# Experts gathered from x by scaled selections, without a normalised copy, in a two-layer decoder trunk

## Chip, cores and metric

One core of a Trainium2 chip runs the whole program in one launch. The metric is the device time of that core in microseconds. TensorE (PE in the profile) multiplies, VectorE (DVE), ScalarE (ACT) and GpSimd (POOL) do the rest, and SyncE (SP) issues the DMAs.

## The reference, cut to what matters

x is 256 tokens by 1024 features, f32, and there are two layers. A layer is a mixer (an input projection, three attention-like branches, gates, an output projection) and then a hierarchical mixture of experts. The change concerns the second part and the memory that the first leaves to it:

```python
def hier_moe_block(x, norm_g, w_rg, b_rg, w_re, b_re, w1, w3, w2):
    xn = rms_norm(x, norm_g).reshape(n_tok, d)
    g_prob = softmax(xn @ w_rg + b_rg);  g_w, g_idx = top_k(g_prob, 1)
    e_in = (xn @ w_re + b_re) of the chosen group (8 of 32 experts)
    e_w, e_idx = top_k(softmax(e_in), 2)
    hid = silu(xn @ w1[e]) * (xn @ w3[e])        # 32 experts, 256 hidden features each
    hid = hid * combine                          # zero where a token did not choose e
    return x + sum over e of hid @ w2[e]
```

So each token goes through two experts of 32, and all 32 experts have their weights read: 3 x 1 MB each, 96 units of 1 MB for a layer.

## The kernel before

**Mixer.** The input and output projections stream 21 x 2 units of mixer weights through three 8 KB places (ring_a). Each unit is two parts; ACT copies a part to a high half (`split` in run_scalar, L1436), DVE subtracts it for the low half (L1725), and PE multiplies three times (L908 to L910, L924 to L926). SP waits for the low halves (`lo_ready`) before it reuses a place.

**Units of the experts.** A unit is w1, w3 or w2 of one expert, 8 KB in each of 128 partitions. `order` (L522 to L596) lists them in the order of use. 25 places hold them: four are used once (`t.once`, for units 4, 5, 23 and 24) and 21 form a ring (`t.ring`). Nearly all lie over buffers of the mixer, so each becomes free at its own moment: over attention scratch, over xnT, over the gates, over the split buffers, over the merged branches, and `once_x` over x itself, when x has been added into the output sums and copied to xn. `units_ahead` in run_sync (L696 to L750) is the hand-written order of these first loads: each has a wait for what frees its place, and they stand in one queue with the mixer's own loads. After that SP loads unit i of the ring when unit i - 21 of the ring has been used (L781 to L783).

**Routing and gathering.** PE and DVE make logits, pick groups and experts (`choose`), and count, so that each token gets a slot number among 32 slots of each expert it chose (`place`). `select_tile` (L2000) compares slot numbers with places: for a batch of 4 experts, a 0/1 matrix of 128 tokens by 4 x 32 slots, for each of two token tiles (tt). It is written twice into `t.sel[:, tt, pair, again, :]`, so that a transpose of both copies puts the same 64 slots into both halves of the partitions, where the scatter wants them. ACT makes the normalised copy of x, permuted so that the features of one k (those that are k modulo 8) lie side by side:

```python
def x_normalised(tt):                                                        # L1602
    act.wait_ge(rs_ready, tt + 1)
    A(t.xn[tt][:, :].rearrange("p (k q) -> p k q", k=NK), t.x[:, tt, :].rearrange("p (q k) -> p k q", k=NK),
      ACT.Copy, scale=t.rs[:, tt:tt + 1]).then_inc(xn_done, 1)
```

PE gathers the rows of a batch with matmuls whose stationary operand is 128 features of xn and whose moving operand is the selection (`first_gather` L1219 for batch 0, `rows` L1249 for the others), and DVE multiplies by norm2_g on the way out (L2054). The order of features fits the weights: a partition of w1 holds eight neighbouring rows.

**The expert loop.** `steps` (L522 to L594) is one order for all engines. For each expert: `hidden` (L1275; w1 and w3 on four column tiles of 32, L1296), ACT's copy of h (L1650), `hT` (L1398; folding and transposing with h[:, j::2] as stationary operand, L1405), silu and the product with the slot weight. For each pair of experts: `outputs` (w2, L1317), a high and a low half of y, `scatter` into the sums of x with selectT (L1365). Between them lie, for each later batch, four gather steps: two of rows (L1253), the slot weights (L1259) and select_T (L1267), and on DVE the selections of the batch after (`select`, `weigh`). PE waits for each unit with `arrived`. x itself is added into the same sums by `x_to_sums` (L1154).

In the trace one f32 matmul shows as two records, a transpose as one: a call of `rows`, 8 matmuls, is 16 records.

Of the kernel before, what the change touches and what calls it, by code (L numbers as in the profile page):

```python
# [48 lines left out]
ONCE_UNITS = (4, 5, 23, 24)  # L49
# [21 lines left out]

STEPS = [("rows", 0), ("rows", 1), ("weights", 0), ("select", 0)]
# [70 lines left out]
def tensors(nc, ctx):  # L143

    class T:
# [10 lines left out]
    once_x = whole.again().sb("unit_over_x", [P, UNIT])  # L156
# [60 lines left out]
    t.xn = [r.sb("xn_first", [P, D])]  # L217
# [3 lines left out]
    t.wif, t.ifT = r.again().sb("w_if", [P, NK, SLOTS]), Region(nc, r.at + 1024, two.end).sb("if_by_feature", [P, SEQ])  # L221
    units_gate = r.sb("unit_over_gates", [P, UNIT])
    t.xs = r.again().sb("scaled_x", [P, NT, D])
# [6 lines left out]
    unit_scores = whole.again().sb("unit_over_smalls_and_scores", [P, UNIT])  # L230
    whole.part(4 * D)

# [5 lines left out]
    t.xn.append(Region(nc, late.at - 4 * D, late.at).sb("xn_second", [P, D]))  # L238
# [5 lines left out]
    t.ring_a_at, t.split_at, t.merged_at = [9, 11, 12], 13, 19  # L244
# [6 lines left out]
    t.ta, t.tb, t.tw = sb("attn_a", [P, 4, 384]), sb("attn_b", [P, 4, 384]), sb("attn_w", [P, 4, 384])  # L251
    r = three.again()
    t.softplus_hi, _, t.softplus_lo = (r.sb(n, [P, 4, 384], F32R) for n in ("softplus_high", "softplus_r", "softplus_low"))
# [9 lines left out]
    r = late.again()  # L263
    t.xT = r.sb("xT_router", [P, NK // 2, SEQ])
# [174 lines left out]
def layer(nc, t, d, l):  # L439
# [51 lines left out]
    xn_done, rounds_ready = S("xn_done"), S("rounds_ready")  # L491
# [10 lines left out]
    x_in_sums, counts_read = S("x_in_sums"), S("counts_read")  # L502
# [179 lines left out]
    def run_sync(sp):  # L682
# [4 lines left out]
        def split_last(u):  # L687

            sp.wait_ge(lo_ready, 2 * (u + 1))
# [6 lines left out]
        def units_ahead(u):  # L696

            if u == MIX_RING + 4:
                experts_begin(sp)
                load_unit(sp, ring_units[0])  # L700
            elif u == 29:
                sp.wait_ge(mb_t, 1)
                load_unit(sp, ring_units[1])
            elif u == 33:
                sp.wait_ge(mb_s, 2)
                load_unit(sp, ring_units[2])
            elif u == 36:
                sp.wait_ge(part_used, PARTS * FIRST_BRANCH)
                load_unit(sp, ring_units[3])
                load_unit(sp, ring_units[4])  # L710
                sp.wait_ge(mb_o, 2)
                sp.wait_ge(d_ready, 1)
                load_unit(sp, ring_units[5])
            elif u == 37:
                sp.wait_ge(ml_s, 1)
                load_unit(sp, ring_units[6])
            elif u == 39:
                sp.wait_ge(ml_pt, 1)
                load_unit(sp, ring_units[7])
            elif u == 40:  # L720
                sp.wait_ge(wr_ready, 2)
                load_unit(sp, ONCE_UNITS[3])
# [156 lines left out]
    def run_tensor(pe):  # L879
# [351 lines left out]
        def gather_first(tt, banks):  # L1231
            pe.wait_ge(sel_ready, tt + 1)
            pe.wait_ge(xn_done, tt + 1)
            first_gather(tt, banks)
# [12 lines left out]
        x_to_sums(0, 1).then_inc(x_in_sums, 1)  # L1247
# [168 lines left out]
    def run_scalar(act):  # L1416
# [37 lines left out]
        def copy(name):  # L1454
# [13 lines left out]
            elif name in ("mbq", "mbk"):  # L1468
                dst = mbqk[:, int(name == "mbk"), :, :]
            elif name in ("mlq", "mlk"):  # L1470
                o = NC * int(name == "mlk")
                dst = mlpre[:, o:o + NC, 3:]
                src = src.rearrange("p b (c n) -> p (b c) n", n=SEQ)
            else:
                o = 0 if name == "mlo" else NC + 4 * int(name[1:])
                dst = gates[:, o:o + 4, :]
                src = src.rearrange("p b (c n) -> p (b c) n", n=SEQ)
# [50 lines left out]
        def sigmoid(a, b, copied):  # L1528
            act.wait_ge(proj_copied, INDEX[copied] + 1)
            A(gates[:, a:b, :], gates[:, a:b, :], ACT.Sigmoid).then_inc(sig, 1)  # L1530
# [32 lines left out]
        sigmoid(0, NC + NK, "g1")  # L1563
        split(2)
        sigmoid(NC + NK, NC + 2 * NK, "g3"); split(2)
        split(1); copy_w(ml_pt, 1, ml_w); split(1)
        act.wait_ge(ml_prod, 1)
        A(brT[0][:, 2], tb[:, :, 0:256], ACT.Copy).then_inc(out_hi, 1)
        split(2); sigmoid(NC + 2 * NK, NC + 3 * NK, "g5")
# [32 lines left out]
        def x_normalised(tt):  # L1602

            act.wait_ge(rs_ready, tt + 1)
            A(t.xn[tt][:, :].rearrange("p (k q) -> p k q", k=NK), t.x[:, tt, :].rearrange("p (q k) -> p k q", k=NK),
              ACT.Copy, scale=t.rs[:, tt:tt + 1]).then_inc(xn_done, 1)

# [4 lines left out]
        x_normalised(0)  # L1612
# [15 lines left out]
        x_normalised(1)  # L1628
# [83 lines left out]
    def run_vector(dve):  # L1712
# [176 lines left out]
        def merge(b, half):  # L1889
# [5 lines left out]
            o = NC + b * NK + 4 * half  # L1895
# [24 lines left out]
        v.tensor_tensor(tb[:, :, 0:256], psA[:, :, 0:256], gates[:, 0:NC, :], ALU.mult).then_inc(ml_prod, 1)  # L1920
        merge(1, 0)
        dve.wait_ge(out_hi, 5)
        v.tensor_tensor(brT[1][:, 2], tb[:, :, 0:256], brT[0][:, 2].bitcast(F32), ALU.subtract).then_inc(ml_e, 1)
# [76 lines left out]
        def select_tile(n, again, tt):  # L2000

            ex = slice(n * BATCH, (n + 1) * BATCH)
            v.tensor_tensor(t.sel[:, tt, :, again, :].rearrange("p q (e s) -> p q e s", e=2),
                            bc(bc(t.slot_no[:, :], 1, 2), 1, HALF),
                            bc(t.place[:, tt, ex].rearrange("p (q e) -> p q e", e=2), 3, SLOTS),
                            ALU.is_equal).then_inc(sel_ready, 1)
# [20 lines left out]
        select_tile(0, 0, 0)  # L2027
# [3 lines left out]
        select_tile(0, 0, 1)  # L2031
        oh1, oh2 = (b[:, :, :].rearrange(four, g=NG) for b in (t.oh1, t.oh2))

        def select(n, again):

            for tt in range(NT):
                select_tile(n, again, tt)

        def weigh(n, chain, first=False):
            ex = slice(n * BATCH, (n + 1) * BATCH)  # L2040
            dve.wait_ge(sel_ready, NT if first else 2 * NT * (n + 1))
            for tt in range(NT):
                v.tensor_tensor(t.selw[:, tt].rearrange("p (q e) s -> p q e s", e=2),
                                t.sel[:, tt, :, 0, :].rearrange("p q (e s) -> p q e s", e=2),
                                bc(t.comb[:, tt, ex].rearrange("p (q e) -> p q e", e=2), 3, SLOTS),
                                ALU.mult).then_inc(selw_ready, 1)
            if first:
                select(n, 1)
                dve.wait_ge(sel_ready, 2 * NT)
# [33 lines left out]
        with dve.Fori(0, rounds) as r:  # L2083
            for what, arg in steps:
                if what == "selection":
# [3 lines left out]
                    if piece < 2:  # L2089
                        select(n, piece)  # L2090
# [32 lines left out]
            with dve.If(r + 1 < rounds):  # L2123
# [3 lines left out]
                select(0, 0)  # L2127
                select(0, 1)
# [89 lines left out]
```

## Time and profile before

| | us |
|---|---|
| median of 3 runs | 967.45 (966.62 to 967.87) |
| the profiled execution, its own time | 970.34 |
| its span, first to last instruction | 968.6 |
| PE busy | 929.8 (96%) |
| PE's weight loads (PEld) busy | 711.8 (73%) |
| DVE busy | 483.4 (50%) |
| ACT busy | 420.0 (43%) |
| POOL busy | 32.1 (3%) |
| HBM read | 291.05 MB |

PE, PEld, DVE, ACT and POOL are shares of time in which an instruction of the engine was under way; matmuls overlap, so PE at 96% need not be PE at its peak. Layer 1's expert stage runs from about 295 to 486 us, layer 2's from about 776 to 965. Lines (L1253) are those of the kernel before.

### The profile page before, as it was taken

The page shows a single profiled execution, that of the slowest core. Times are in us where ns is not written, and L with a number is a line of the kernel's source. Part 1 is how long each engine was busy: PE and PEld are TensorE (multiplying, and loading weights), DVE is VectorE, ACT ScalarE, POOL GpSimd, SP SyncE. Part 2 cuts the span into 40 slices and gives each one's busy share as a digit, 9 for nine tenths or more (in the row PEclk, how much of TensorE's full clock was granted, in tenths as well). Part 3 has the DMA queues.
Part 4 walks back from the last instruction along what each step waited for, and adds up shares of the span by engine and source line. Part 5 has one row for each costly group of instructions (what it writes and reads, how often), then busy time and mean ns, then how long its engine had stood idle before and what let it go on. Part 6 is the DMA issues. An engine that isn't in the chain of part 4 may idle for free.

```text
span 968.6 us, 17435 instructions
## 1 busy us (share of the span) xinstructions
PE 929.8 (96%) x7170; PEld 711.8 (73%) x7170; DVE 483.4 (50%) x912; ACT 420.0 (43%) x649; POOL 32.1 (3%) x56
## 2 busy tenths in 40 slices
PE   8999999999999999977899999999999999999876
PEld 8898888788796566644598988887887966655543
DVE  6565884577854222222173659755787532223111
ACT  6556654657552221111185566555764522212111
POOL 1010100000000000000010110000000000000000
PEclk9999999999999999999899999999999999999989
DMA  8845455558989999999967255565579899999996
GB/s 269 300 132 174 142 197 168 198 186 323 398 330 390 426 425 425 426 426 426 389 214 260 91 177 179 174 217 181 207 320 398 336 395 425 426 426 425 426 426 259
DMA packets 86304, 293.25 MB, mean 303 GB/s; under 512 B 17040, under 2 KB 17104, under 8 KB 61904
## 3 DMA queue, kind: packets, MB, share of 16 engines
q1 hardware_dynamic: 86224, 292.12, 78.1%
q8 instruction: 58, 0.95, 0.4%
q14 instruction: 22, 0.18, 0.0%
HBM read 291.05 MB, written 1.05 MB: 302 GB/s over the span
## 4 chain that ended last, share of the span: by engine, by line
PE 84%; DMA 12%; ACT 2%; DVE 1%; issue 1%; SPq 0%; POOL 0%; ACTq 0%; DVEq 0%
PE ps_a L908 11%; PE ps_a L910 11%; PE ps_a L909 11%; PE ps_b L1296 10%; DMA unit_over_gates<-in_w_dram 5%; PE ps_b L1317 4%; PE ps_b L1253 4%; PE ps_a L924 4%; PE ps_a L925 4%; PE ps_a L926 4%; DMA units_over_merged<-in_w_dram 3%; PE ps_b L1405 3%; DMA units_over_xnT<-in_w_dram 3%; PE ps_a L1365 3%; PE ps_b L1152 1%; PE ps_b L992 1%
## 5 line engine op out<-in xcount | busy, mean ns | idle before, releaser
L1436 ACT ACTIVATE w_high<-weight_ring 128x1024 fp32r<-128x1024 f32 x166 | 173.9, 1058 | 168.2 <-PE ps_a L910 128.4
L1725 DVE TENSOR_TENSOR w_low<-weight_ring,w_high 128x1024 fp32r<-128x1024 f32 x167 | 200.9, 1229 | 91.6 <-ACT w_high L1436 91.2
L908 PE MATMUL ps_a<-w_high,xnT_high 128*128 128x512 f32 x352 | 140.0, 398 | 0.0
L909 PE MATMUL ps_a<-w_low,xnT_high 128*128 128x512 f32 x352 | 137.2, 390 | 0.0
L910 PE MATMUL ps_a<-w_high,xnT_low 128*128 128x512 f32 x352 | 137.2, 390 | 0.0
L924 PE MATMUL ps_a<-xnT_high,w_high 128*128 128x256 f32 x320 | 91.1, 285 | 0.1
L925 PE MATMUL ps_a<-xnT_low,w_high 128*128 128x256 f32 x320 | 90.5, 283 | 0.0
L926 PE MATMUL ps_a<-xnT_high,w_low 128*128 128x256 f32 x320 | 90.5, 283 | 0.0
L1650 ACT ACTIVATE h<-ps_b 128x256 f32<-128x256 f32 x64 | 24.6, 384 | 143.7 <-PE ps_b L1296 143.7
L908 PEld LDWEIGHTS ps_a<-w_high,xnT_high 128*128 128x128 f32 x352 | 66.1, 188 | 16.2 <-issue 2.8
L910 PEld LDWEIGHTS ps_a<-w_high,xnT_low 128*128 128x128 f32 x352 | 66.1, 188 | 14.1
L909 PEld LDWEIGHTS ps_a<-w_low,xnT_high 128*128 128x128 f32 x352 | 66.1, 188 | 13.4 <-issue 0.5
L2115 DVE TENSOR_TENSOR y_lo<-ps_b,y_hi 128x512 fp32r<-128x512 f32 x30 | 20.7, 691 | 103.4 <-ACT y_hi L1682 103.4
L1405 PEld LDWEIGHTS ps_b<-fold_two_matrices,h 128*128 128x128 f32 x256 | 35.0, 196 | 37.9 <-issue 33.7
L924 PEld LDWEIGHTS ps_a<-xnT_high,w_high 128*128 128x128 f32 x320 | 61.4, 192 | 0.4 <-issue 0.3
L925 PEld LDWEIGHTS ps_a<-xnT_low,w_high 128*128 128x128 f32 x320 | 61.4, 192 | 0.0
L926 PEld LDWEIGHTS ps_a<-xnT_high,w_low 128*128 128x128 f32 x320 | 61.4, 192 | 0.0
L2054 DVE TENSOR_TENSOR XT<-ps_b,gain_by_weight_row 128x512 f32<-128x512 f32 (+1 forms) x32 | 21.6, 675 | 79.6 <-PE ps_b L1253 77.8
L2105 DVE TENSOR_TENSOR h_weighted<-ps_b,slot_weight 128x64 f32<-128x64 f32 x64 | 14.0, 219 | 88.6 <-ACT silu_h L1676 88.6
L1682 ACT ACTIVATE y_hi<-ps_b 128x512 fp32r<-128x512 f32 x30 | 17.9, 598 | 79.4 <-PE ps_b L1317 79.4
L1296 PE MATMUL ps_b<-units_over_splits,XT 128*32 128x256 f32 x512 | 41.8, 411 | 5.6 <-DMA units_over_splits<-in_w_dram 5.6
L1253 PE MATMUL ps_b<-select,xn_first 128*128 128x128 f32 x224 | 47.0, 292 | 0.0
(384 smaller groups left out, 1720.4 us busy)
## 6 DMA issues: line engine op xcount, KB each, us to landing
weight_ring<-in_w_in_dram SPq DMA_DIRECT2D x62, 1024.0 KB, 5.1
units_over_splits<-in_w_dram SPq DMA_DIRECT2D x48, 1024.0 KB, 23.0
units_over_attention<-in_w_dram SPq DMA_DIRECT2D x40, 1024.0 KB, 21.0
weight_ring<-in_w_dram SPq DMA_DIRECT2D x24, 1024.0 KB, 18.9
units_over_xnT<-in_w_dram SPq DMA_DIRECT2D x20, 1024.0 KB, 20.8
units_over_merged<-in_w_dram SPq DMA_DIRECT2D x16, 1024.0 KB, 24.0
weight_ring<-in_w_branch_dram SPq DMA_DIRECT2D x12, 1024.0 KB, 5.1
unit_from_layer_begin<-in_w_dram SPq DMA_DIRECT2D x10, 1024.0 KB, 19.0
```

Source lines behind the costliest of these rows:

```text
L908: mm(pair[:, tt, :], xh, hi[:, k, :], start=row == 0, stop=False)
L909: mm(pair[:, tt, :], xh, lo[:, k, :], start=False, stop=False)
L910: last = mm(pair[:, tt, :], xl, hi[:, k, :], start=False, stop=row == rows - 1)
L924: mm(dst, wh, xh, start=row == 0 and s % 2 == 0, stop=False, skip_group_check=True)
L925: mm(dst, wh, xl, start=False, stop=False, skip_group_check=True)
L926: last = mm(dst, wl, xh, start=False, stop=row == rows - 1, skip_group_check=True)
L1253: last = mm(bank[:, i * P:(i + 1) * P], t.xn[tt][:, k * P:(k + 1) * P], t.sel[:, tt, :, 0, :], start=tt == 0, stop=tt == NT - 1)
L1296: ins = mm(ps_h[c * SLOTS:(c + 1) * SLOTS, :], xT[:, k, slots], units[w][:, k, :], start=i == 0, stop=i == rows_each - 1, skip_group_check ...
L1317: ins = mm(ps_y[c * SLOTS:(c + 1) * SLOTS, :], t.hid[p % 2][:, e, j, :], w2, start=j == 0, stop=j == 1, skip_group_check=True)
L1405: last = mm(ps_x[:, o:o + 2 * SLOTS], t.h[:, j:FE:2], t.fold_two[:, :], start=True, stop=True)
L1436: A(mix_buf(whi, i), mix_raw(i), ACT.Copy).then_inc(hi_ready, 1)
L1725: v.tensor_tensor(mix_buf(wlo, i), mix_raw(i), mix_buf(whi, i).bitcast(F32), ALU.subtract).then_inc(lo_ready, 1)
```

## The change

What it does:

- **No xn.** `x_normalised`, both xn buffers (4 KB each) and the semaphore `xn_done` go. The gathers take `t.x[:, tt, k:D:NK]` as stationary operand, every eighth feature of a row.
- **Scaled selections.** The copy with index 0 of a selection now holds the token's rstd in place of 1: four tensor_scalars of 128x32 (compare, then multiply by rs) for each tile. The copy with index 1 stays 0/1; `weigh` and `select_T` use that one. In batch 0 the 0/1 copy is made before `weigh`'s products, no longer after them.
- **select_T.** Only one copy can be transposed now, so each half of the partitions gets its own matmul with the identity: eight matmuls with 64 columns instead of four transposes of 128.
- **Places.** x must stay, so `once_x` goes, with the wait for `x_in_sums`. The freed 8 KB become a ring place, `unit_merged`, over the gates of merged_by_token: 3 places used once and 22 in the ring, 25 as before. Unit 23 is now loaded as the last of the ring's first lap. `unit_over_scores` moves 4 KB on and waits for `ml_o`; the gates, w_if, ml's product, attn_b and attn_w, and scaled_x lie at other addresses; the last sigmoid becomes two ACTIVATEs.

```diff
-ONCE_UNITS = (4, 5, 23, 24)
+ONCE_UNITS = (4, 5, 24)
+GATES_AT = [NC, NC + 4, NC + 12, NC + 16, NC + 8, NC + 20]
...
-    t.xn = [r.sb("xn_first", [P, D])]
...
+    r = Region(nc, gates_at + UNIT * 4, two.end + 4 * D)
+    unit_merged = r.sb("unit_over_merged_by_token", [P, UNIT])
     units_gate = r.sb("unit_over_gates", [P, UNIT])
...
-    t.once = [once_y[:, :], once_XT1[:, :], once_x[:, :], once_choice[:, :]]
+    t.once = [once_y[:, :], once_XT1[:, :], once_choice[:, :]]
...
-              t.ring_a[:, 2, :]]
+              t.ring_a[:, 2, :], unit_merged[:, :]]
...
             elif u == 39:
-                sp.wait_ge(ml_pt, 1)
+                sp.wait_ge(ml_o, 1)
                 load_unit(sp, ring_units[7])
...
                 load_unit(sp, ring_units[9])
-                sp.wait_ge(merged_lo, 2)
+                sp.wait_ge(merged_lo, 1)
                 load_unit(sp, ONCE_UNITS[1])
                 split_last(40)
                 load_unit(sp, ring_units[11])
+                sp.wait_ge(merged_lo, 2)
+                load_unit(sp, ring_units[13])
                 split_last(41)
                 load_unit(sp, ring_units[12])
...
-                sp.wait_ge(x_in_sums, 1)
-                sp.wait_ge(xn_done, NT)
-                sp.wait_ge(sq_done, 5)
-                load_unit(sp, ONCE_UNITS[2])
...
-                    last = mm(first_bank(k), t.xn[tt][:, k * P:(k + 1) * P], t.sel[:, tt, :, 0, :],
+                    last = mm(first_bank(k), t.x[:, tt, k:D:NK], t.sel[:, tt, :, 0, :],
...
-                    last = mm(bank[:, i * P:(i + 1) * P], t.xn[tt][:, k * P:(k + 1) * P], t.sel[:, tt, :, 0, :],
+                    last = mm(bank[:, i * P:(i + 1) * P], t.x[:, tt, k:D:NK], t.sel[:, tt, :, 0, :],
...
-                    last = tr(bank[:, o:o + P], t.sel[:, tt, j].rearrange("p d s -> p (d s)"), t.ident[:, :])
+                    for half in range(2):
+                        last = mm(bank[half * 2 * SLOTS:(half + 1) * 2 * SLOTS, o:o + P], t.sel[:, tt, j, 1, :],
+                                  t.ident[:, :], start=True, stop=True, skip_group_check=True)
...
-        split(2); sigmoid(NC + 2 * NK, NC + 3 * NK, "g5")
+        split(2); sigmoid("g5", *((GATES_AT[g], GATES_AT[g] + 4) for g in (4, 5)))
...
-        def select_tile(n, again, tt):
+        def select_tile(n, scaled, tt):
...
+            if scaled:
+                for i in range(BATCH):
+                    e = n * BATCH + i
+                    ins = v.tensor_scalar(t.sel[:, tt, i // 2, 0, i % 2 * SLOTS:(i % 2 + 1) * SLOTS], t.slot_no[:, :],
+                                          t.place[:, tt, e:e + 1], t.rs[:, tt:tt + 1], ALU.is_equal, ALU.mult)
...
         def weigh(n, chain, first=False):
             ex = slice(n * BATCH, (n + 1) * BATCH)
-            dve.wait_ge(sel_ready, NT if first else 2 * NT * (n + 1))
+            if first:
+                select(n, False)
+            dve.wait_ge(sel_ready, 2 * NT * (n + 1))
...
-                                t.sel[:, tt, :, 0, :].rearrange("p q (e s) -> p q e s", e=2),
+                                t.sel[:, tt, :, 1, :].rearrange("p q (e s) -> p q e s", e=2),
```

## Rows read from the trace of the kernel before

**Rows 1.** page, part 2: what the DMA moved, GB/s in 40 slices of the span
```profile
GB/s 269 300 132 174 142 197 168 198 186 323 398 330 390 426 425 425 426 426 426 389 214 260 91 177 179 174 217 181 207 320 398 336 395 425 426 426 425 426 426 259
```

**Rows 2.** busy us by stage: window, length, PE, PEld, DVE, ACT, POOL, PEclk, DMA, GB/s
```profile
305.00:400.00 95.00, 95.00 (x1048) 58.93 (x1044) 27.27 (x86) 19.09 (x53) 0.00 (x0) 1.00 1.01 425
400.00:474.90 74.90, 62.09 (x633) 37.95 (x632) 13.81 (x45) 11.93 (x33) 0.00 (x0) 0.93 1.01 425
...
880.00:954.10 74.10, 62.34 (x636) 38.72 (x635) 13.81 (x45) 12.24 (x34) 0.00 (x0) 0.93 1.01 425
```

**Rows 3.** chain of waits in the expert stages: start us, us, what
```profile
305.33 1.98 PE ps_b L1253 x16
...
403.94 26.37 DMA unit_over_gates<-in_w_dram
...
460.30 3.22 PE ps_b L1296 x32
...
470.15 1.86 PE ps_b L1296 x32
...
474.94 2.02 PE ps_b L1317 x16
...
909.41 3.00 PE ps_b L1296 x32
```

**Rows 4.** waits of PE, 395 to 480: us in total, times, longest
```profile
PE ps_b L1405 <- ACT h L1650: 0.6, 1, 0.6
```

**Rows 5.** weight loads by line: ns min/median/max, first and last start, form
```profile
L1253 PEld LDWEIGHTS ps_b<-select,xn_first x224: 186/192/333, 305.3 to 930.9; 128*128 128x128 f32 x112
...
L994 PEld LDWEIGHTS ps_b<-attn_w,sb_v x32: 137/137/138, 75.7 to 595.5; 128*64 128x64 f32 x32
...
L1296 PEld LDWEIGHTS ps_b<-weight_ring,XT x192: 106/110/110, 313.3 to 916.5; 128*32 128x32 f32 x192
...
L1405 PEld LDWEIGHTS ps_b<-fold_two_matrices,h x256: 192/196/197, 297.9 to 956.4; 128*128 128x128 f32 x128
```

**Rows 6.** groups by line and form, ACT and DVE: busy us, mean ns, idle before
```profile
L1605 ACT ACTIVATE xn_first<-x_res,rstd 128x1024 f32<-128x1024 f32 x2 | 4.4, 2212 | 0.1
...
L1498 ACT ACTIVATE scaled_x<-mb_qk 128x1024 f32<-128x1024 f32 x4 | 4.0, 1047 | 0.0
...
L407 DVE TENSOR_REDUCE fold<-ident 128x32 f32<-128x128 f32 x1 | 0.4, 370 | 0.0
...
L2003 DVE TENSOR_TENSOR select<-slot_no,place 128x128 f32<-128x128 f32 x64 | 16.0, 287 | 1.1
```

**Rows 7.** a small DVE group; PE's timeline before the second count
```profile
L2050 DVE TENSOR_SCALAR place<-place 128x8 f32<-128x8 f32 x16 | 2.6, 166 | 0.1
...
290.96 0.19 PE L1206 MATMUL ps_b<-assigned,ones_bf 128*128 128x32 bf16 x1 [0.21 <-DVE assigned L1991]
```

**Rows 8.** PE's timeline, values weighed by head, select_T: start us, us, line
```profile
75.43 0.66 PE L992 MATMUL ps_b<-attn_w,sb_v 128*64 128x256 f32 x4
...
76.93 0.50 PE L908 MATMUL ps_a<-w_high,xnT_high 128*128 128x512 f32 x1
...
297.61 0.60 PE L1267 MATMUL ps_b<-ident,select 128*128 128x128 f32 x4
298.04 0.58 PE L1405 MATMUL ps_b<-fold_two_matrices,h 128*128 128x64 f32 x4
```

**Rows 9.** SP's timeline of DMA issues around the start of the expert stage
```profile
267.74 6.04 SPq L625 DMA_DIRECT2D weight_ring<-in_w_dram  x2
...
295.29 0.33 SPq L625 DMA_DIRECT2D unit_over_x<-in_w_dram  x1
297.18 0.33 SPq L625 DMA_DIRECT2D unit_from_layer_begin<-in_w_dram  x1
```

**Rows 10.** the stretch before the expert stage, both layers; columns of rows 2
```profile
273.00:281.00 8.00, 8.00 (x58) 7.36 (x57) 1.96 (x4) 4.39 (x10) 0.00 (x0) 1.00 0.67 218
753.00:761.00 8.00, 8.00 (x56) 7.30 (x55) 2.18 (x4) 4.39 (x11) 0.00 (x0) 1.00 0.65 223
```

More of the change, by code:

```diff
@@ L155, in tensors @@
     sb = whole.sb
-    once_x = whole.again().sb("unit_over_x", [P, UNIT])
     t.x = sb("x_res", [P, NT, D])
@@ L220, in tensors @@
     t.selT = [r.sb(f"selectT{i}", [P, HALF, SEQ], F32R) for i in range(2)]
-    t.wif, t.ifT = r.again().sb("w_if", [P, NK, SLOTS]), Region(nc, r.at + 1024, two.end).sb("if_by_feature", [P, SEQ])
+    at = gates_at + 12 * SEQ * 4
+    t.wif, t.ifT = Region(nc, at, two.end).sb("w_if", [P, NK, SLOTS]), Region(nc, at + 1024, two.end).sb("if_by_feature", [P, SEQ])
+    r = Region(nc, gates_at + UNIT * 4, two.end + 4 * D)
+    unit_merged = r.sb("unit_over_merged_by_token", [P, UNIT])
     units_gate = r.sb("unit_over_gates", [P, UNIT])
-    t.xs = r.again().sb("scaled_x", [P, NT, D])
+    t.xs = Region(nc, r.at - 4 * D, two.end).sb("scaled_x", [P, NT, D])
     once_y = r.again().sb("unit_over_y", [P, UNIT])
@@ L250, in tensors @@
     sb = three.again().sb
-    t.ta, t.tb, t.tw = sb("attn_a", [P, 4, 384]), sb("attn_b", [P, 4, 384]), sb("attn_w", [P, 4, 384])
+    t.ta, t.tw, t.tb = sb("attn_a", [P, 4, 384]), sb("attn_w", [P, 4, 384]), sb("attn_b", [P, 4, 384])
     r = three.again()
-    t.softplus_hi, _, t.softplus_lo = (r.sb(n, [P, 4, 384], F32R) for n in ("softplus_high", "softplus_r", "softplus_low"))
+    t.softplus_hi, t.softplus_lo = (r.sb(n, [P, 4, 384], F32R) for n in ("softplus_high", "softplus_low"))
     sb = spare.sb
@@ L263, in tensors @@
     r = late.again()
+    t.product = r.again().sb("ml_product", [P, NC, SEQ])
     t.xT = r.sb("xT_router", [P, NK // 2, SEQ])
@@ L1246, in run_tensor @@
         x_to_sums(0, 0, [1])
-        x_to_sums(0, 1).then_inc(x_in_sums, 1)
+        x_to_sums(0, 1)
         def rows(bank, q):
@@ L1526, in if_softplus, with sigmoid @@
             A(lft[:, :, :], lft[:, :, :], ACT.Ln, bias=1.0).then_inc(if_sp, 1)
-        def sigmoid(a, b, copied):
+        def sigmoid(copied, *ranges):
             act.wait_ge(proj_copied, INDEX[copied] + 1)
-            A(gates[:, a:b, :], gates[:, a:b, :], ACT.Sigmoid).then_inc(sig, 1)
+            for a, b in ranges:
+                last = A(gates[:, a:b, :], gates[:, a:b, :], ACT.Sigmoid)
+            last.then_inc(sig, 1)
         split(4); copy("sbq"); split(4); copy("sbk"); split(4); copy("sbv")
@@ L1562, in run_scalar @@
         rows_exp(d_ready, 1, False, w_ready)
-        sigmoid(0, NC + NK, "g1")
+        sigmoid("g1", (0, NC + NK))
         split(2)
-        sigmoid(NC + NK, NC + 2 * NK, "g3"); split(2)
+        sigmoid("g3", (GATES_AT[2], GATES_AT[3] + 4)); split(2)
         split(1); copy_w(ml_pt, 1, ml_w); split(1)
         act.wait_ge(ml_prod, 1)
-        A(brT[0][:, 2], tb[:, :, 0:256], ACT.Copy).then_inc(out_hi, 1)
-        split(2); sigmoid(NC + 2 * NK, NC + 3 * NK, "g5")
+        A(brT[0][:, 2], t.product[:, :, :], ACT.Copy).then_inc(out_hi, 1)
+        split(2); sigmoid("g5", *((GATES_AT[g], GATES_AT[g] + 4) for g in (4, 5)))
         nc.scalar.preload_act_table_set(EXP_LN)
@@ L1600, in run_scalar @@
               ACT.Copy).then_inc(xT_act, 1)
[L1602 to L1606, printed above, removed]
         experts_begin(act)
@@ L1611, in run_scalar @@
         rstd(0, msum_ready, rs_ready)
-        x_normalised(0)
         def exps(tt):
@@ L1627, in run_scalar @@
         rstd(1, msum_ready, rs_ready)
-        x_normalised(1)
         exps(1)
@@ L1919, in run_vector @@
         dve.wait_ge(ml_o, 1)
-        v.tensor_tensor(tb[:, :, 0:256], psA[:, :, 0:256], gates[:, 0:NC, :], ALU.mult).then_inc(ml_prod, 1)
+        v.tensor_tensor(t.product[:, :, :], psA[:, :, 0:256], gates[:, 0:NC, :], ALU.mult).then_inc(ml_prod, 1)
         merge(1, 0)
         dve.wait_ge(out_hi, 5)
-        v.tensor_tensor(brT[1][:, 2], tb[:, :, 0:256], brT[0][:, 2].bitcast(F32), ALU.subtract).then_inc(ml_e, 1)
+        v.tensor_tensor(brT[1][:, 2], t.product[:, :, :], brT[0][:, 2].bitcast(F32), ALU.subtract).then_inc(ml_e, 1)
         split(2); merge(1, 1)
@@ L1998, in place @@
                                             in1=t.A[:, tt, :], op0=ALU.add, op1=ALU.mult))
-        def select_tile(n, again, tt):
[L2002 to L2006, printed above, removed]
+        def select_tile(n, scaled, tt):
[4 more added lines that the diff above has]
+                                          t.place[:, tt, e:e + 1], t.rs[:, tt:tt + 1], ALU.is_equal, ALU.mult)
+            else:
+                ex = slice(n * BATCH, (n + 1) * BATCH)
+                ins = v.tensor_tensor(t.sel[:, tt, :, 1, :].rearrange("p q (e s) -> p q e s", e=2),
+                                      bc(bc(t.slot_no[:, :], 1, 2), 1, HALF),
+                                      bc(t.place[:, tt, ex].rearrange("p (q e) -> p q e", e=2), 3, SLOTS),
+                                      ALU.is_equal)
+            ins.then_inc(sel_ready, 1)
         third, last = slice(CHUNK, CHUNK + 256), slice(CHUNK + 256, D)
@@ L2026, in run_vector @@
         place(0)
-        select_tile(0, 0, 0)
+        select_tile(0, True, 0)
         ch.until(logits_out(1))
@@ L2030, in run_vector, with select @@
         place(1)
-        select_tile(0, 0, 1)
+        select_tile(0, True, 1)
         oh1, oh2 = (b[:, :, :].rearrange(four, g=NG) for b in (t.oh1, t.oh2))
-        def select(n, again):
+        def select(n, scaled):
             for tt in range(NT):
-                select_tile(n, again, tt)
+                select_tile(n, scaled, tt)
         def weigh(n, chain, first=False):
             ex = slice(n * BATCH, (n + 1) * BATCH)
-            dve.wait_ge(sel_ready, NT if first else 2 * NT * (n + 1))
+            if first:
+                select(n, False)
+            dve.wait_ge(sel_ready, 2 * NT * (n + 1))
             for tt in range(NT):
                 v.tensor_tensor(t.selw[:, tt].rearrange("p (q e) s -> p q e s", e=2),
-                                t.sel[:, tt, :, 0, :].rearrange("p q (e s) -> p q e s", e=2),
+                                t.sel[:, tt, :, 1, :].rearrange("p q (e s) -> p q e s", e=2),
                                 bc(t.comb[:, tt, ex].rearrange("p (q e) -> p q e", e=2), 3, SLOTS),
                                 ALU.mult).then_inc(selw_ready, 1)
-            if first:
-                select(n, 1)
-                dve.wait_ge(sel_ready, 2 * NT)
             chain.after(v.tensor_scalar(t.place[:, :, ex], t.place[:, :, ex], -float(SLOTS), None, ALU.add))
@@ L2089, in run_vector @@
                     if piece < 2:
[L2090 removed]
+                        select(n, piece == 0)
                     else:
@@ L2126, in run_vector @@
                 dve.sem_clear(go_dve)
-                select(0, 0)
-                select(0, 1)
+                select(0, True)
+                select(0, False)
                 first_rows()
```

16 lines of the change are left out of this document (7 added, 9 removed).

## The prediction

> **What bounds the kernel now.** I read the slices of the page first, then the chain of waits, then the engines' busy time by stage. The slices show two stages for each layer: a mixer, in which the DMA moves 130 to 270 GB/s, and an expert stage, in which it moves 425 GB/s from end to end [rows 1]. In the first 95 us of the expert stage both PE and the DMA are full; in its last 75 us the DMA still moves 425 GB/s, while PE is busy for 62.1 us of 74.9 (62.3 of 74.1 in layer 2) [rows 2]. The chain agrees: it leaves PE at 403.94 for transfers and comes back to PE for good only at 460, after which the last w2 units are fetched [rows 3]. So PE first lives on the units loaded ahead, uses them up, and then takes each unit as it lands. The end of the stage is set by the moment at which the DMA has moved 96 units of 1.05 MB, and PE has about 13 us in hand. How much exactly: idle 74.9 - 62.1 = 12.8 us, less 0.6 us in which it waits for ACT's copy of h [rows 4], plus 1.4 us that one group of hidden matmuls loses to a lower granted clock after an idle stretch (3.22 us, where such a group takes 1.86; 3.00 in layer 2) [rows 3]. That is 13.6 us in layer 1 and 11.8 - 0.6 + 1.1 = 12.3 us in layer 2. A change gains here if it makes DMA work start sooner, and costs nothing until it has added those 13 us to PE's work. This change does some of both.
>
> **The stationary operand read with a stride.** Every gather of rows (L1253, L1226) now loads 128 values that lie 32 bytes apart in x, where xn had them side by side. Nothing in the trace loads PE in that way, so I bound it. A load of 128 columns takes 192 ns, of 64 columns 137, of 32 columns 110 [rows 5]: 0.85 ns a column beside a fixed part, 109 ns in all, and a call of 16 records takes 1.98 us, 124 ns each [rows 3], so the load paces the record and whatever it grows by is added in full. Lower end: no growth. Upper end: h is loaded with every second value (8 bytes apart) and takes 196 ns, 4 more [rows 5]; two of its values share 16 bytes, so a fresh 16 bytes cost at most 113 / 64 = 1.77 ns, and 128 of them 226 ns, 117 more than now. Two neighbours show what such a stride costs other engines. ACT's x_normalised reads x with just this stride: 2212 ns, where a copy of 1024 values side by side takes 1047, so 1.14 ns more for each value. DVE's reduction that builds fold reads values 128 bytes apart: 370 ns for 128 values, where another pass over 128 takes 287, so 0.65 ns more [rows 6]. Both pay, and h's 4 ns are what 1.77 ns for each fresh 16 bytes would give. I take 0.8 ns a value, between DVE's and the upper end (0.91): 102 ns for each record. Per layer there are 7 batches of 2 calls of 16 records, 224 x 0.102 = 22.8 us. The first batch's 32 records stand before the stage on PE's path: 3.3 us, of which the 0.2 us that PE waits before L1206 now hides some [rows 7]: 3.1.
>
> The Trainium skill speaks against this change too: "Advanced Engine Details and Errata", section "SBUF Cachelines", says that SBUF is read in 16-byte lines, that two hits on a line are needed to hide its latency, and that a new line with each access is penalised. It gives no size. By that rule the loads get dearer; were it not to hold for PE's weight loads, the second case below would be the forecast. The ACT and DVE rows agree with it, and no row before the change shows it for PE.
>
> **select_T.** Four transposes become eight matmuls of 64 columns, 16 records. Today's four take 0.43 us from start to next start. The nearest rows are the 16 records of L992 and L994, of the same 128*64 form on alternating halves, with 8 x 256 + 8 x 128 = 3072 columns in 1.50 us, 0.49 ns a column [rows 8]; 16 x 128 columns give 1.0 us. That is 0.57 us more for each of 8 batches, 4.6 us a layer. Ends: 0.3 us if the halves overlap better, 1.3 us if they don't overlap at all.
>
> **DVE.** A scaled tile is four tensor_scalars where one tensor_tensor of 287 ns [rows 6] was. A small tensor_scalar takes 166 ns [rows 7], pipelined less: 0.4 to 0.7 us for the four, so 0.1 to 0.4 more before PE's first gathers. The unscaled selections of batch 0 now stand before weigh, 0.5 us, and slot_weights waits for them right after the first hidden group. Together 0.5 us on PE's path. In the loop the six further instructions run while PE does a hidden group of 1.86 us; uncovered they would cost 0.5 us a batch.
>
> **At nothing.** x_normalised (2 x 2.2 us of ACT a layer) goes: the first is done long before its use, the second ends while DVE still chooses; what is late next is the selection. One more ACT instruction for g5 falls into idle time before the next split. The unit over the scores waits for ml_o instead of ml_pt; two w_out transfers issued just ahead cover that, and without them 1 to 2 us of DMA idle would come out of the second case's gain alone.
>
> **The extra place.** A unit goes out at 268 instead of unit_over_x at 295.29 [rows 9]. From 273 to 281 the DMA has a busy share of 0.67 (0.65 in layer 2), so 2.6 to 2.8 us idle [rows 10]; one unit is 1.05 MB at 425 GB/s, 2.5 us, and fits. Against it, nothing is queued between the last merged unit and the first reused place at 297.18, 1.9 us later than x's unit [rows 9]: 0 to 1.9 us of idle come back; I take 0.8. Net 1.7 us a layer, if the DMA still sets the end.
>
> **The sum.** PE's added work a layer: 22.8 + 3.1 + 4.6 + 0.5 = 31.0 us. That is more than PE has in hand, so the DMA's gain is worth nothing and PE sets the end: 31.0 - 13.6 = 17.4 and 31.0 - 12.3 = 18.7, together 36 us. The profiled execution took 970.34 us, 2.9 over the median of the runs shown, so 1006.4 by its own time and **1003 us** by the median.
>
> **The cases.** About 0.2% (1.9 us) can be told from no change.
> 1. Strided loads pay about double (0.50): 1003. Its own range is 988 to 1012: 83 ns a record (DVE's extra) and 0.3 us for select_T give 23.9 us a layer at the lower end, 117 ns a record 34.9 at the upper (halves that don't overlap would add 6 us a layer to that).
> 2. Strided loads are free (0.34), the case on the other side. PE's extra is 4.6 + 0.5 us, below the 12 to 13 in hand, the DMA sets the end, and the filled gap is worth 1.7 us a layer: 964. It decides as long as a record grows by less than (12.3 - 5.1) / 256 = 28 ns. For it: a load asks for a value each 0.85 ns, which may be slow enough to hide a fresh line each time, and h pays 4 ns only. Against it: the ACT and DVE rows.
> 3. Free loads and no gain (0.08): the idle time at 273 comes back in full where unit_over_x was (1.9 us), or behind the wait for ml_o: 967.
> 4. Loads dearer by about 55 ns (0.08): 14.1 + 5.1 = 19.2 us, less what is in hand, +5.6 and +6.9: 980.
>
> Faster 0.34, same 0.08, slower 0.58. The range for 8 in 10 must take in the first two: 963 to 1010; a little of the free case lies below it, and the dearest form of the first above.
>
> **What would show it.** Right: PE's weight loads of x_res for the gather near 290 ns instead of 192, a call of 16 records near 3.6 us, PE without waits for transfers after 400, and the DMA's share falling below 1 well before the stage ends. Wrong: loads of 192 to 220 ns; then PE still waits for units from about 400 on, the DMA's idle time at 273 is gone, and the last w2 group starts 1 to 2 us sooner in each layer. select_T near 1 us would confirm its term, 1.7 us would say that the halves don't overlap. Wrong in another way: PE waits before its first gathers of more than 0.5 us, or a wait for the selections in the loop.

## The result, and the profile after

The changed kernel takes 1030.14 us (median of 4 runs, 1028.46 to 1030.49) beside 967.25 for the kernel before (4 runs, 966.62 to 967.87): 1.0647 times as long, 95% interval 1.0633 to 1.0660. The direction was predicted, the size was not: 62.9 us slower where 36 were forecast, and outside the range. The profiled execution took 1030.34 us, its span is 1028.6.

PE now reads x with the stride. The loads and matmuls of the gather in the expert stage, over both layers, against the 192 ns of L1253 [rows 5]; then PE's waits over the span, longest sums first (us in total, times, longest):

```profile
L1251 PEld LDWEIGHTS ps_b<-select,x_res x448: 312/336/340, 311.2 to 993.5; 128*128 128x128 f32 x150
L1251 PE MATMUL ps_b<-select,x_res x448: 401/402/505, 311.2 to 993.7; 128*128 128x128 f32 x150
```

```profile
PE ps_b L1251 <- DVE select L1999: 10.9, 12, 0.9
PE ps_b L1383 <- DVE hid L2109: 2.9, 2, 1.5
PE ps_b L1405 <- ACT h L1644: 2.3, 4, 0.6
...
PE ps_b L1225 <- DVE select L1999: 1.2, 4, 0.3
```

A load takes 336 ns, 144 more. A call of 16 records grows by 2.03 us (1.98 before [rows 3], 4.01 where nothing waits ahead of it, as at 344.88 below), 127 ns a record. Nothing waits for a transfer of weights any more; in its place stands a wait for DVE's scaled selections, 0.9 us in 12 of the 14 batches gathered in the loops. The chain of waits shows what surrounds one of them (start us, us, what):

```profile
332.27 0.63 PE ps_b L1405 x4
...
332.92 0.23 ACT silu_h L1670
...
333.25 0.24 DVE h_weighted L2105
...
333.51 0.24 DVE hid L2109
...
333.77 1.76 DVE select L1999 x8
335.53 0.14 issue
335.66 4.16 PE ps_b L1251 x16
339.82 2.58 PE ps_b L1317 x16
...
344.88 4.01 PE ps_b L1251 x16
```

DVE first has to finish the expert of the moment (h_weighted, hid), and only then makes eight selections of 0.22 us each. PE's hidden group runs meanwhile, from 332.8 to 334.75, and is over 0.8 us before the last of them. The gather's call behind the wait takes 4.16 us, and the w2 group behind it 2.58 us. That second number is the clock. Stretches of 2.5 us of the same batch, and the stages (columns of rows 2):

```profile
335.00:337.50 2.50, 1.84 (x8) 1.87 (x8) 0.52 (x3) 0.28 (x1) 0.00 (x0) 1.00 1.02 426
337.50:340.00 2.50, 2.50 (x14) 2.23 (x17) 0.14 (x1) 0.00 (x0) 0.00 (x0) 0.57 1.01 426
340.00:342.50 2.50, 2.50 (x17) 0.48 (x10) 0.55 (x1) 0.00 (x0) 0.00 (x0) 0.74 1.02 433
342.50:345.00 2.50, 2.50 (x37) 1.50 (x37) 1.54 (x5) 0.72 (x2) 0.00 (x0) 1.00 1.01 426
...
337.90:341.20 3.30, 3.30 (x16) 2.03 (x19) 0.69 (x1) 0.00 (x0) 0.00 (x0) 0.50 1.00 425
...
273.00:281.00 8.00, 8.00 (x60) 7.43 (x58) 1.57 (x4) 2.75 (x8) 0.00 (x0) 1.00 0.89 349
281.00:305.00 24.00, 23.24 (x174) 19.94 (x177) 12.40 (x83) 5.27 (x17) 0.00 (x0) 0.93 0.71 270
305.00:400.00 95.00, 91.68 (x866) 60.57 (x859) 26.39 (x93) 15.52 (x43) 0.00 (x0) 0.95 0.99 409
400.00:505.60 105.60, 102.28 (x977) 68.28 (x977) 25.70 (x88) 16.79 (x48) 2.32 (x2) 0.95 0.88 364
...
1000.00:1015.00 15.00, 14.42 (x176) 9.91 (x176) 1.95 (x7) 2.92 (x8) 0.00 (x0) 1.00 0.00 1
```

After 11 of the 12 waits (not after the first of layer 2), about 2 us into the strided call, the granted clock falls to half (0.50, the level of 1.2 GHz) for over 3 us; here from 337.9 to 341.2. It is at half once more just ahead of the stage, from 290.1 to 293.4 in layer 1. The DMA's share in the second part of the stage is 0.88, where it was 1.01 [rows 2], and from 1000 to 1015, in the last 30 us of layer 2, it moves next to nothing: the end is PE's. The gap at 273 is mostly filled (0.89 for 0.67 [rows 10]).

### The profile page after: what moved, and what is told of

It reads as the page before. It is cut to its first block, busy times and chain, and to the rows that moved or that the text cites. A ratio compares the mean times of both kernels' runs of the same rounds, so it can differ in the third digit from the quotient of the medians.

```text
span 1028.6 us, 17905 instructions
## 1 busy us (share of the span) xinstructions
PE 1002.1 (97%) x7362; PEld 779.3 (76%) x7362; DVE 503.9 (49%) x1008; ACT 411.1 (40%) x647; POOL 31.1 (3%) x56
## 4 chain that ended last, share of the span: by engine, by line
PE 92%; DVE 4%; ACT 2%; issue 1%; DMA 1%; POOL 0%; SPq 0%; ACTq 0%; DVEq 0%
PE ps_b L1251 11%; PE ps_a L907 11%; PE ps_a L909 10%; PE ps_a L908 10%; PE ps_b L1296 9%; PE ps_b L1317 6%; PE ps_a L923 4%; PE ps_a L924 4%; PE ps_a L925 4%; PE ps_b L1405 4%; PE ps_a L1365 3%; DVE select L1999 2%; PE ps_b L1225 2%; PE ps_b L1266 2%; PE ps_b L1151 1%; PE ps_b L1257 1%
## 5 line engine op out<-in xcount | busy, mean ns | idle before, releaser
L1251 PEld LDWEIGHTS ps_b<-select,x_res 128*128 128x128 f32 x448 | 108.9, 334 | 23.8 <-issue 22.1
L1251 PE MATMUL ps_b<-select,x_res 128*128 128x128 f32 x448 | 115.0, 417 | 10.9 <-DVE select L1999 10.9
L1670 ACT ACTIVATE silu_h<-ps_b 128x64 f32<-128x64 f32 x64 | 14.3, 223 | 102.8 <-PE ps_b L1405 102.8
## 6 DMA issues: line engine op xcount, KB each, us to landing
weight_ring<-in_w_dram SPq DMA_DIRECT2D x24, 1024.0 KB, 10.9
```

Of the source, the lines that this page charges most:

```text
L1251: last = mm(bank[:, i * P:(i + 1) * P], t.x[:, tt, k:D:NK], t.sel[:, tt, :, 0, :], start=tt == 0, stop=tt == NT - 1)
```

## Experiments

Each comparison has its own runs of the kernel before: 967.57 us (13 runs) for the first four below, 966.83 (15 runs) for the adjacent kernel with one-pass selections and for the three that move the order to the weights, 967.16 (11 runs) for the three between them.

**The changed kernel without the stride.** It gathers 128 adjacent features of x, so other ones than the reference's.

```diff
-    t.x[:, tt, k:D:NK]
+    t.x[:, tt, k * P:(k + 1) * P]
```

> The changed kernel, but its gathers take 128 features of x that lie side by side, so other features than those the weights want. Theory S (the stride of the stationary operand is the cost): a weight load is back at 192 ns and a call of 16 records at 2.0 us. PE then has only select_T (about 4.7 us a layer), the waits for the four tensor_scalars (5.5 us a layer) and a later start (2 us) on top of before, about the 12 to 13 us that it had in hand, so the DMA or PE sets the end by a hair: 963 to 971 us. Rival X (the gathers are slow because of what they read or multiply, x's buffer or the rstd in the selections, not because of the stride): loads stay at 335 ns and the time near 1030 us.

Measured: 969.08 us, 1.0018 (1.0004 to 1.0032). All but 2 us of the 63 go with the stride, and yet PE waits for DVE as often and as long as in the changed kernel. Waits of PE from 303 to 500 us:

```profile
PE ps_b L1251 <- DVE select L1999: 5.5, 6, 0.9
PE ps_b L1296 <- DMA units_over_splits<-in_w_dram: 2.4, 1, 2.4
...
```

These waits come out of what PE has in hand, and so cost next to nothing here (with one-pass selections and no such waits the time is the same, below). That is also why this run alone can't price the stride: it removes the cause that makes everything else count.

**The kernel before with the stride.** `t.xn[tt][:, k:D:NK]` in both gathers, all else as before; other features than the reference's.

> The kernel before, but its gathers take every eighth value of xn, so other features than those the weights want; nothing else of the change. Theory S: each call of 16 records takes 4.0 us in place of 1.98, 14 x 2.0 + 2 x 2.2 = 32.5 us a layer, less the 13 that PE has in hand: +39 us, 1006 us. If the clock also falls after each strided call without any wait for DVE ahead of it, 4 to 5 us a layer more: 1015 us. Rival X: no change in the loads and 967 us.

Measured: 999.51 us, 1.0325 (1.0304 to 1.0346). PE's added work is 28 calls of 2.03 us and the first gathers, which let the stage begin 3.4 us later (298.63 for 295.26): 56.8 + 6.8 = 63.6 us. The time rose by 31.9, so PE had 31.7 us in hand, 15.8 a layer, where 13 were expected. The granted clock is 1.00 from 330 to 480: strided calls alone don't bring it down.

**The law of the stride.** In the kernel before, block k of the gather in the loop is read at a stride of k + 1 values, each from its own line (L1255 for stride 1 to L1269 for stride 8); other features than the reference's.

```diff
-    t.xn[tt][:, k * P:(k + 1) * P]
+    t.xn[tt][:, 0:127 * (k + 1) + 1:k + 1]
```

> The kernel before, with feature block k of each later batch read from xn at a stride of k + 1 values (4 to 32 bytes), a line of the source for each, so that each line's load time can be read; other features than the weights want. Theory S with 16-byte lines: 192 ns at a stride of 1, 196 at 2, between at 3, and about 335 ns alike at 4 to 8, since each value then lies in a 16-byte line of its own. Rival: the load grows in proportion to the distance, about +20 ns for each step. Rival: it doubles already at 2 or 3.

Measured: 973.44 us (one run). Weight loads from xn_second, ns min/median/max:

```profile
L1255 PEld LDWEIGHTS ps_b<-select,xn_second x28: 192/192/192, 305.2 to 927.0; 128*128 128x128 f32 x28
L1257 PEld LDWEIGHTS ps_b<-select,xn_second x28: 196/196/197, 305.7 to 927.4; 128*128 128x128 f32 x28
L1259 PEld LDWEIGHTS ps_b<-select,xn_second x28: 261/261/261, 306.3 to 928.1; 128*128 128x128 f32 x28
L1261 PEld LDWEIGHTS ps_b<-select,xn_second x28: 330/330/330, 307.1 to 928.9; 128*128 128x128 f32 x28
L1263 PEld LDWEIGHTS ps_b<-select,xn_second x28: 314/314/314, 310.4 to 934.4; 128*128 128x128 f32 x28
L1265 PEld LDWEIGHTS ps_b<-select,xn_second x28: 318/318/318, 311.3 to 935.2; 128*128 128x128 f32 x28
L1267 PEld LDWEIGHTS ps_b<-select,xn_second x28: 326/326/326, 312.2 to 936.2; 128*128 128x128 f32 x28
L1269 PEld LDWEIGHTS ps_b<-select,xn_second x28: 334/335/336, 313.2 to 937.1; 128*128 128x128 f32 x28
```

A stride of two values (8 bytes) costs 4 ns, three cost 69 ns, and from four (16 bytes) on the load is at 314 to 335 ns. It doesn't grow in proportion to the distance: what counts most is how many values lie in the same 16 bytes. The spread of 21 ns among the strides from four up is not explained by that. The time agrees with the stock of 32 us: the two calls of a batch take 2.74 and 3.84 us from start to next start, 2.62 more than 2 x 1.98, which is 36.7 us for 14 batches, and the kernel got 5.9 us slower, so 30.8 us were hidden. (The mean extra of the eight loads is 91 ns, and 448 of that would be 41 us: the calls grow by nine tenths of what the loads grow.)

**The changed kernel with one-pass selections.** The scaled copy is made of the 0/1 copy by one multiplication of 128x128 with rs for each tile: four DVE instructions a batch where there were ten. Everything is computed.

```diff
-                for i in range(BATCH):
...
-                    ins = v.tensor_scalar(t.sel[:, tt, i // 2, 0, i % 2 * SLOTS:(i % 2 + 1) * SLOTS], t.slot_no[:, :],
-                                          t.place[:, tt, e:e + 1], t.rs[:, tt:tt + 1], ALU.is_equal, ALU.mult)
+            dve.wait_ge(sel_ready, count)
+            v.tensor_scalar(t.sel[:, tt, :, 0, :], t.sel[:, tt, :, 1, :], t.rs[:, tt:tt + 1], None, ALU.mult)
```

> The changed kernel, but the scaled selection of a tile is made from the 0/1 one by one multiplication of 128x128 by rstd, not by four comparisons of 128x32. Theory D (the tensor_scalars of 0.22 us each make PE wait, and each wait with the strided call behind it brings PE's clock down once a batch): the 5.5 us of waits and the six or seven stretches at the lower clock (0.7 us each) go in each layer, 18 to 20 us in all: 1011 us. Rival: the new chain of comparison and multiplication is as late as the old one, or the clock falls from the strided call alone: 1020 to 1030 us.

Measured: 1008.91 us, 1.0435 (1.0410 to 1.0459), 21.2 us less than the changed kernel, with the stride in place. A batch in its chain:

```profile
331.38 1.86 PE ps_b L1296 x32
333.24 0.05 issue
333.30 4.04 PE ps_b L1251 x16
337.34 1.85 PE ps_b L1317 x16
...
354.25 1.02 PE ps_b L1266 x16
```

No wait for the selections, w2 groups at 1.85 us, mean clock 1.000 over the span. So the small selections cost 21 us once PE sets the end: 10.9 us of waits, 11 times the 0.85 us of a fallen clock (4.16 - 4.04 and 2.58 - 1.85), 9.4 us, and 1.8 us at the start of the two stages (the first hidden group begins at 300.1 for 298.9 in layer 1; in layer 2 at 809.4 for 797.2, of which 11.65 come from layer 1), 22.1 in all. Over the strided kernel before it stands 9.4 us. select_T is 7.3 us of that: a call takes 1.02 us here, and there 0.59 us in 14 calls of 16 and 0.44 in the first of each layer. One of the 14, in the chain of the strided kernel before:

```profile
327.57 0.59 PE ps_b L1267 x4
```

The other 2.1 us are not accounted for; the runs of either kernel spread over 3.3 us.

**Adjacent and one pass: what is left is the place.** Both edits above together; other features than the reference's.

> The changed kernel with both suspected costs taken away at once: each gather reads 128 adjacent features of x (so other features are gathered than the reference wants), and the scaled selection of a batch is one 128x128 multiplication of the 0/1 one per token tile. What is left of the change is the ninth unit place, the missing copy and the longer select_T. Theory A (stride 61 us, DVE selections the rest, the place worth about 1.7 us a layer where the queue sets the end): no wait of PE for DVE select, the waits for DMA units back, 964 to 965 us. Theory B (the place is worth nothing, since select_T and the fuller ring only move the wait): 967 to 968 us. If the DVE waits cost nothing in the adjacent form either, it reads 969 like the adjacent kernel with eight small selections.

Measured: 968.07 us, 1.0014 (1.0005 to 1.0024). No gain, though the gap at 273 is filled. The next two runs say why.

**The kernel before, profiled again.**

> The kernel before, profiled a second time. Its first profiled execution lies 2.9 us over the median of its times, so places gained and lost by a few us can't be read against it. Theory A (the extra place is worth 1.7 us a layer, the profile of the adjacent form with two-pass selections shows it): the last w_dram unit of the first expert stage lands near 460 here too. Theory B (the first profiled execution was a slow one, and the place is worth nothing): it lands at 458 to 459, and the time is 966 to 968 us.

Measured: 966.35 us (one run). So its first profiled execution was on the long side, and small differences are to be read against this one. The two stretches around the place, of this kernel:

```profile
273.00:281.00 8.00, 8.00 (x58) 7.39 (x57) 1.78 (x4) 4.42 (x9) 0.00 (x0) 1.00 0.68 219
281.00:305.00 24.00, 23.20 (x236) 17.77 (x234) 12.99 (x84) 9.54 (x23) 0.00 (x0) 1.00 0.98 386
```

and of the adjacent kernel with one-pass selections:

```profile
273.00:281.00 8.00, 8.00 (x57) 7.35 (x57) 1.91 (x4) 3.06 (x9) 0.00 (x0) 1.00 0.88 360
281.00:305.00 24.00, 23.39 (x241) 18.26 (x243) 12.95 (x84) 6.15 (x20) 0.00 (x0) 1.00 0.91 351
```

DMA idle before: 8 x 0.32 + 24 x 0.02 = 3.0 us. After: 8 x 0.12 + 24 x 0.09 = 3.1 us. What is won at 273 is idle again where unit_over_x used to be fetched: from 295 to 300 the DMA's share is 0.55, and 0.92 in the kernel before. There are 25 places before and after; the change moves one of them.

**One place fewer.** The same kernel without `unit_merged` in the ring, 24 places; other features than the reference's.

```diff
-              t.ring_a[:, 2, :], unit_merged[:, :]]
+              t.ring_a[:, 2, :]]
...
-                load_unit(sp, ring_units[13])
```

> The adjacent form with two-pass selections, with the new place (the unit over merged by token, issued at 268) taken out again, so that no unit is loaded into the memory of the missing copy at all; features other than the reference's are gathered. Theory A (where the queue sets the end, a place filled before the stage is worth up to its transfer of 2.5 us a layer): 971 to 973 us. Theory B (places are worth nothing here): 967 to 968 us, as with it.

Measured: 973.04 us, 1.0058 (1.0041 to 1.0076). By the ratios that is 0.0044 x 967 = 4.3 us over the kernel with the place, 2.1 a layer:

```profile
273.00:281.00 8.00, 8.00 (x59) 7.39 (x58) 1.72 (x4) 2.91 (x8) 0.00 (x0) 1.00 0.69 253
281.00:305.00 24.00, 23.39 (x240) 18.08 (x242) 12.96 (x84) 6.33 (x21) 0.00 (x0) 1.00 0.86 347
```

8 x 0.31 + 24 x 0.14 = 5.8 us idle, 2.7 more. A place more or less is worth about its transfer of 2.5 us a layer (the intervals of the two ratios leave the 2.1 uncertain by about 1); the place moved here is worth nothing.

**Stride and small selections in the kernel before.** The strided kernel before, its scaled selections made by eight tensor_scalars (compare, multiply by one); select_T, the copy and the places stay. Other features than the reference's.

> The kernel before with its gathers strided (every eighth feature of the normalised copy) and its scaled selections made by eight tensor_scalars of 128x32 a batch; select_T, the copy and the places stay as before. Other features than the reference's are gathered. Theory A (each batch's wait of 0.9 us for these selections, and the fall of PE's clock when such a wait meets a strided call, are what the two-pass form gained): 1018 to 1022 us, 20 us over the strided kernel before, PE waits of 0.9 us for DVE select, and windows with a granted clock near 0.5 to 0.6 after them. Theory B (the waits alone): 1010 us, clock at 1.00 through the loop.

Measured: 1022.43 us, 1.0567 (1.0539 to 1.0594), 22.9 us over the strided kernel before. The waits are the same, 5.5 us in 6 pieces in layer 1, and the clock falls again, though only from the third such wait of a layer on. Twelve waits are 11.0 us and eight falls of 0.85 us are 6.8; the other 5 us were not broken down. Stretches behind the first such wait and the third (columns of rows 2):

```profile
335.00:337.50 2.50, 2.50 (x12) 2.50 (x12) 0.00 (x0) 0.00 (x0) 0.00 (x0) 1.00 1.01 426
...
387.50:390.00 2.50, 2.50 (x12) 2.50 (x11) 0.00 (x0) 0.00 (x0) 0.00 (x0) 0.82 1.00 423
390.00:392.50 2.50, 2.50 (x14) 0.62 (x17) 0.69 (x1) 0.00 (x0) 0.00 (x0) 0.50 1.00 413
```

The adjacent kernel has the waits without the stride, and its clock stays at 1.00 through them (here the wait and the two stretches behind it):

```profile
370.00:372.50 2.50, 1.59 (x27) 0.88 (x20) 1.96 (x9) 0.38 (x1) 0.00 (x0) 1.00 1.00 413
372.50:375.00 2.50, 2.50 (x26) 1.78 (x29) 0.69 (x1) 0.00 (x0) 0.00 (x0) 1.00 1.01 426
375.00:377.50 2.50, 2.50 (x36) 1.25 (x32) 0.70 (x2) 0.73 (x2) 0.00 (x0) 1.00 1.01 426
```

So these waits alone don't bring the clock down (none of 12), nor do strided calls alone; together they do, in 19 cases of 24, in two kernels of otherwise different make. What sets the five others apart is not shown. A longer wait needs no stride: behind its wait of 2.4 us for a transfer the adjacent kernel is at 0.50 too, from 459.3 to 462.7.

**Moving the order to the weights.** Three kernels that compute everything and read x cheaply; w2 is loaded as it was. Row 128 k + p of w1 and w3 goes to partition p, with adjacent gathers; then the same with one-pass selections; then pairs of rows, with gathers at the cheap stride of two and one-pass selections.

```diff
+            sp.dma_start(unit_buf(n).rearrange("p (k n) -> p k n", k=NK),
+                         src.rearrange("(k p) n -> p k n", p=P)).then_inc(unit_in[place_of(n)], 16)
...
+            sp.dma_start(unit_buf(n).rearrange("p (g m) -> p g m", g=NK // 2),
+                         src.rearrange("(g p j) n -> p g (j n)", p=P, j=2)).then_inc(unit_in[place_of(n)], 16)
```

> The changed kernel with the feature order moved from the gather to the weights: w1 and w3 are loaded with row 128 k + p in partition p (pieces of 1 KB in place of 8 KB for a partition), and block k of the gather then reads 128 adjacent features of x. Everything that the reference computes is computed. Theory A (pieces of 1 KB move at the 425 GB/s of the larger ones, the stride was the cost): as the adjacent form, 969 us. Theory B (smaller pieces cost the queue bandwidth): the loop is bound by DMA, and a rate of 380 GB/s for two thirds of its units would add 8% of some 190 us a layer's loop, 980 us or more, with the mean GB/s of the loop below 425.

> As the kernel with w1 and w3 loaded as 128 k + p, and the scaled selection made by one 128x128 multiplication of the 0/1 one. Everything that the reference computes is computed. Theory A: equal to the adjacent form with the same selections, 964 to 965 us, faster than both kernels. Theory B (1 KB pieces are slower): DMA bound, 980 us or more, no gain from the selections since DMA sets the end.

> A middle way: w1 and w3 are loaded with rows 256 g + 2 p and 256 g + 2 p + 1 in partition p (pieces of 2 KB), and the gather reads every second feature of x; the scaled selection is one 128x128 multiplication. Everything that the reference computes is computed. Theory A (a load at stride 2 takes 196 ns against 192 in the sweep of strides, and 2 KB pieces move at full rate): 964 to 965 us. Theory B (any stride or any smaller piece costs): above the 1 KB form by the stride if that is at fault, below it if the pieces are.

Measured: 994.38 us (1.0283, 1.0268 to 1.0299), 993.20 (1.0271, 1.0254 to 1.0288) and 977.37 (1.0111, 1.0094 to 1.0127). All of them are bound by the DMA, which no longer reaches 425 GB/s. The first stretch of the stage with pieces of 1 KB:

```profile
305.00:400.00 95.00, 91.37 (x1036) 56.24 (x1032) 30.06 (x102) 18.94 (x52) 0.00 (x0) 1.00 1.06 395
```

and with pieces of 2 KB:

```profile
305.00:400.00 95.00, 94.78 (x1058) 59.37 (x1052) 25.27 (x81) 18.99 (x53) 0.00 (x0) 1.00 1.04 410
```

The DMA engines are busy all the time in both, at 395 and 410 GB/s. In the first of the three, PE still waits 4.7 us in layer 1 for the selections; taking these waits away (the second) saves nothing clear of noise. The pairs are the best full version without the copy, 53 us under the changed kernel and still 11 over the kernel before. No run beat the kernel before.

## Why the prediction was right and wrong

- **PE sets the end, the DMA doesn't**: right. So was the reading that PE's reserve swallows the first part of any addition.
- **The strided load**: the mechanism was right, the size was not. The term of 102 ns a record, between 0 and an upper end of 117, measured 127. The upper end came from h's 4 ns by one cost for each fresh 16 bytes, 1.77 ns. In the sweep the strides from four values up cost 138, 122, 126, 134 and 143 ns more; with the prediction's 83 ns of fixed part that is 1.80 to 1.97 ns for each fresh 16 bytes when every value needs one. The row that had the size of the load was ACT's copy, 1.14 ns more a value; PE's load pays 144 / 128 = 1.13. That the two have the same cause is not shown. I had chosen 0.8, between DVE's row and my upper end. A second error went the other way: the load's growth was to be added in full, but a load grows by 144 ns and its record by 127. The Trainium skill ("Advanced Engine Details and Errata", section "SBUF Cachelines") gives the rule of 16-byte lines, with two hits wanted on each, for no engine by name and without a size. The sweep agrees for PE's loads, 4 ns more with two values in 16 bytes and 122 to 143 with one. In the sum: 28 calls x 2.03 = 56.8 us where 45.6 stood, 11.2 more.
- **First gathers**: 3.4 us a layer, predicted 3.1. Right.
- **select_T**: 1.02 us for 16 records, predicted 1.0. But the call it replaces was read from the first one of a layer, 0.43 us; the others take 0.59. So the term is 7.3 us, not 9.2.
- **DVE in the loop at nothing**: this is the step that took the time out of the range. I covered the selections with a hidden group of 1.86 us. But a gather waits for eight of them, 1.76 us, and DVE comes to them only after h_weighted and hid of the expert just done, when 1.0 us of the hidden group is left. In the kernel before, the same place in DVE's order held two selections, 0.49 us. The price named if the cover was gone was 0.5 us a batch; it is 0.9: 10.9 us in all. The kernel with one-pass selections, with every strided load at its full price and without these waits, took 1008.91 us, which lies inside 963 to 1010. At the start of the two stages the selections cost 1.8 us, predicted 1.0. A wait for the selections in the loop was named beforehand as a sign of being wrong.
- **The clock**: not foreseen, 11 x 0.85 = 9.4 us. It comes with the waits and goes with them.
- **PE in hand**: 25.9 us predicted, 31.7 by the strided kernel before. The prediction counted a lower clock only for one hidden group a layer, 1.4 and 1.1 us. The kernel before spends more time at it in layer 1:

```profile
415.20:418.50 3.30, 2.96 (x29) 1.57 (x32) 0.00 (x0) 0.00 (x0) 0.00 (x0) 0.50 1.01 425
446.00:449.30 3.30, 3.30 (x32) 1.69 (x24) 0.00 (x0) 0.16 (x1) 0.00 (x0) 0.50 1.01 427
459.60:462.90 3.30, 2.60 (x28) 1.41 (x32) 0.00 (x0) 0.00 (x0) 0.00 (x0) 0.50 1.00 425
```

In layer 2 it is at 0.50 for as long (910.2 to 913.4, 923.8 to 930.5). At half the clock up to half of 9.9 us is lost, 5.0 a layer, so up to 12.2 + 5.0 and 11.2 + 5.0, 33.4 us, were in hand. That is an estimate and an upper end; the 31.7 lies between it and the 25.9.

- **The extra place**: its term would have been wrong. 1.7 us a layer were forecast where the DMA sets the end; the runs give none, as in the third case of the forecast. It had no part in the time here.

The sum with what was measured: 56.8 + 6.8 + 7.3 + 1.8 + 10.9 + 9.4 = 93.0, less 31.7, is 61.3 us; the kernel got 62.9 us slower, so 1.6 are left over. The 31.7 is itself what the strided kernel before left of its first two terms, so the sum tests the other four. The prediction's own 62 - 26 = 36 lacks 11.2 of load and 20.3 of waits and clock, has 0.5 too much in small terms, and 5.8 too little in hand: 25.2 up to the 61.3.

## What to carry to other kernels

A weight load of 128x128 fp32 whose values lie 16 bytes or more apart took PE 64 to 74% longer here, and every matmul whose pace the load sets pays nine tenths of that. So a layout copy off the critical path, on an engine with idle time, can be cheap for what it saves; 8 bytes apart cost 2%. Before an engine's added work is written off as hidden, look up in the chain what it must finish first, and not only how long the cover is. And count places before and after: one that is filled earlier only helps if the later fetch doesn't go away with it.

## What was not expected of the hardware

- A weight load of 128x128 fp32 at strides of 1 to 8 values: 192, 196, 261, 330, 314, 318, 326, 335 ns. That four is dearer than five was seen in both buffers, and wasn't followed up.
- The granted clock falls to half for over 3 us after a wait of 0.9 us if a call of 4 us with strided loads follows, in 19 of 24 cases; after the same wait with a call of 2 us in none of 12, and in the 28 strided calls of each of the two kernels without such waits in none. Why it spared the first two such waits of each layer in one kernel, and only one of twelve in the other, is open.
- The DMA moves 425 GB/s with 8 KB in a row for each partition, 410 when two units of three come in pieces of 2 KB and 395 with pieces of 1 KB, its engines busy throughout.
